# RWKV-7 + NSA trunk on one core: kk's head sums, their spread back and the gate branch's last 32 rows as 32-wide tiles on quarters of the array

## The reference, cut to what matters

```python
r = xr @ w_r;  k = xk @ w_k;  v = xv @ w_v
w_log = -softplus(-(w0 + tanh(xw @ wa) @ wb)) - 0.5
a = sigmoid(a0 + (xa @ aa) @ ab)
g = sigmoid(xg @ ga) @ gb                       # ga: 1024 x 160, gb: 160 x 1024
kk = heads(k * k_k)                             # 16 heads of 64
kk = kk / max(norm(kk over the head), 1e-12)
k = k * (1 + (a - 1) * k_a)
```

## Time and profile before

| | |
|---|---|
| median of 3 executions | 880.41 us (880.11 to 882.34) |
| the profiled execution | 882.25 us, of which the span in the trace is 880.5 us |
| PE busy | 809.8 us, 92% of the span |
| DVE / ACT / POOL busy | 75% / 48% / 16% |
| twelve projections and what stands between them | about 47 to 151 us of the span |
| scan over time | from about 151 us on |

### The profile page before, as it was taken

The page is one execution under the profiler, slowest core; times in us unless marked ns, Lnnn a source line. Parts: engine busy times, 40 slices in busy tenths (PEclk is TensorE's granted clock), DMA queues, the critical chain, the costliest instruction groups (busy, mean ns, idle before and its releaser), DMA issues.

```text
span 880.5 us, 17952 instructions
## 1 busy us (share of the span) xinstructions
PE 809.8 (92%) x7613; PEld 699.9 (79%) x7613; DVE 663.1 (75%) x727; ACT 420.2 (48%) x596; POOL 138.4 (16%) x207
## 2 busy tenths in 40 slices
PE   0899999899989899999999989998889899999997
PEld 0598899787877599999998788975566799999975
DVE  4897987998977689999997674789854687555552
ACT  2269532654553734434444654238646454444441
POOL 8700014534621300000000041101110000000000
PEclk9999999999999999999999999989999999999999
DMA  8953225423250859999993586670005276655541
GB/s 312 335 167 112 85 97 172 176 99 113 99 205 1 311 211 374 378 377 376 377 366 123 192 254 202 187 256 1 1 2 190 99 283 241 192 191 191 191 144 48
DMA packets 71838, 170.18 MB, mean 193 GB/s; under 512 B 5432, under 2 KB 6736, under 8 KB 71760
## 3 DMA queue, kind: packets, MB, share of 16 engines
q1 hardware_dynamic: 68784, 160.75, 52.2%
q0 software_dynamic: 2416, 7.15, 2.7%
q10 hardware_dynamic: 560, 1.14, 0.3%
HBM read 166.42 MB, written 1.05 MB: 190 GB/s over the span
## 4 chain that ended last, share of the span: by engine, by line
PE 66%; DVE 22%; ACT 7%; issue 3%; DMA 2%; ACTq 0%; POOL 0%; DVEq 0%; POOLq 0%
PE ps L1724 8%; PE ps L1727 8%; PE ps L1726 8%; PE ps L1735 7%; PE ps L1737 7%; PE ps L1739 7%; DVE wlo L1070 4%; PE ps L1670 2%; PE ps L1672 2%; PE ps L1673 2%; DVE acc L1042 2%; ACT whi L638 2%; PE ps L1841 2%; DVE hfull L1354 1%; DVE tt L1241 1%
## 5 line engine op out<-in xcount | busy, mean ns | idle before, releaser
L1070 DVE TENSOR_TENSOR wlo<-raw,whi 128x2048 fp32r<-128x2048 f32 (+1 forms) x98 | 217.2, 2216 | 55.4 <-ACT whi L638 53.2
L638 ACT ACTIVATE whi<-raw 128x2048 fp32r<-128x2048 f32 (+1 forms) x98 | 179.8, 1843 | 135.1 <-DMA raw<-in_mlp_down_dram 87.5
L1724 PE MATMUL ps<-ghi,whi 128*128 128x256 f32 x576 | 164.8, 286 | 8.0 <-ACT ghi L884 4.3
L1726 PE MATMUL ps<-glo,whi 128*128 128x256 f32 x576 | 164.4, 285 | 0.0
L1727 PE MATMUL ps<-ghi,wlo 128*128 128x256 f32 x576 | 164.3, 285 | 0.0
L1724 PEld LDWEIGHTS ps<-ghi,whi 128*128 128x128 f32 x576 | 111.9, 194 | 11.3 <-issue 7.6
L1726 PEld LDWEIGHTS ps<-glo,whi 128*128 128x128 f32 x576 | 112.1, 195 | 0.5
L1727 PEld LDWEIGHTS ps<-ghi,wlo 128*128 128x128 f32 x576 | 112.0, 194 | 0.0
L1735 PE MATMUL ps<-whi,hidhi 128*128 128x512 f32 x256 | 100.8, 394 | 2.0 <-DVE wlo L1070 2.0
L1737 PE MATMUL ps<-whi,hidlo 128*128 128x512 f32 x256 | 99.8, 390 | 0.0
L1739 PE MATMUL ps<-wlo,hidhi 128*128 128x512 f32 x256 | 99.6, 389 | 0.0
(11 more groups left out here) (358 smaller groups left out, 1593.4 us busy)
## 6 DMA issues: line engine op xcount, KB each, us to landing
raw<-in_mlp_up_dram SPq DMA_DIRECT2D x32, 1024.0 KB, 5.5
raw<-in_mlp_down_dram SPq DMA_DIRECT2D x32, 1024.0 KB, 5.2
raw<-in_ada_w_dram SPq DMA_DIRECT2D x24, 1024.0 KB, 6.0
late<-in_ada_w_dram SPq DMA_DIRECT2D x24, 1024.0 KB, 9.0
late<-in_kv_ada_w_dram SPq DMA_DIRECT2D x8, 1024.0 KB, 8.3
raw<-in_kv_w_dram SPq DMA_DIRECT2D x6, 1024.0 KB, 5.3
raw<-in_rw_k_dram SPq DMA_DIRECT2D x4, 1024.0 KB, 8.8
raw<-in_rw_r_dram SPq DMA_DIRECT2D x4, 1024.0 KB, 5.0
```

Of the source, the lines that this page charges most:

```text
L638: ins = sc.activation(whi[i][:, ks, :], raw[i][:, :].rearrange("p (k n) -> p k n", k=4)[:, ks, :], ACT.Copy)
L1070: ins = dv.tensor_tensor(wlo[i][:, ks, :], raw[i][:, :].rearrange("p (k n) -> p k n", k=4)[:, ks, :], whi[i][:, ks, :].bitcast(F32), ALU.s ...
L1724: mm(out_, whi[b][:, k, cols], hi[:, k0 + k, :], start=(first and k == 0 and m % 2 == 0), stop=False, skip_group_check=True)
L1726: mm(out_, whi[b][:, k, cols], lo[:, k0 + k, :], start=False, stop=False, skip_group_check=True)
```

## The change

It touches four small products and the tables that they use:

- the head sums go to four column tiles of 32 (output partitions 0, 32, 64, 96): pair j of heads goes with the table `indq` (128 x 2 x 32) to tile j // 2, so four tiles take two matmuls each, ordered by quarters (0, 2, 4, 6, 1, 3, 5, 7);
- root, clamp and reciprocal work on 128 partitions instead of 16;
- the spread takes 32 rows of `s16` per matmul (row tiles), in the same order; `indt` becomes 128 x 2 x 128;
- `gate_inner` computes the last 32 rows four times, once into each quarter of bank 5: 32 matmuls instead of 8;
- `gate_outer` replaces `lora_outer` for the gate: first the 8 matmuls with gb0, then 8 with 32 rows of gb1 each, a quarter of the array each; gb1 is loaded four times, once into each quarter (four DMAs instead of one);
- the memsets of s16, tg1 and gb1 go, and SyncE's wait for s_const ahead of gb0 goes; low_rank(0) and gate_inner wait for 8 small loads instead of 5.

```diff
-        indt = at("indt", [P, D], F32, 196.5)
+        indt = at("indt", [P, 2, P], F32, 196.5)
+        indq = at("indq", [P, 2, 32], F32, 197.5)
...
-                    sp.wait_ge(s_const, 1)
                     sp.dma_start(gb0[:, :], A["rw_gb"][0, 0:P, :]).then_inc(s_lora_out, 16)
-                    sp.dma_start(gb1[0:32, :], A["rw_gb"][0, P:160, :]).then_inc(s_lora_out, 16)
+                    for c in range(4):
+                        sp.dma_start(gb1[32 * c:32 * c + 32, :], A["rw_gb"][0, P:160, :]).then_inc(s_lora_out, 16)
...
-            st.do(g.memset(s16[:, :], 0.0))
-            st.do(g.memset(tg1[:, :], 0.0))
-            st.do(g.memset(gb1[:, :], 0.0))
...
+            st.do(g.memset(indq[:, :, :], 0.0))
...
+                st.do(g.memset(indq[rows, :, :].rearrange("p j c -> p (j c)")[:, e:e + 35:34], 1.0))
...
-            st.do(g.memset(indt[:, :], 1.0))
-            select(indt[:, :], 0, [[1, D]], -64)
-            select(indt[:, :], 63, [[-1, D]], 64)
+            st.do(g.memset(indt[:, :, :], 0.0))
+            for c in range(4):
+                select(indt[32 * c:32 * c + 32, :, :].rearrange("p j (e d) -> p j e d", e=2), 0,
+                       [[-2, 2], [-1, 2], [0, N]], 1, ALU.not_equal, 1.0)
...
-            sc.activation(tg1[0:32, :], ps[0:32, 5, 0:S], ACT.Sigmoid).then_inc(s_t1, 1)
+            sc.activation(tg1[:, :], ps[:, 5, 0:S], ACT.Sigmoid).then_inc(s_t1, 1)
...
-            sc.activation(s16[0:H, :], ps[0:H, 6, 0:S], ACT.Sqrt).then_inc(s_kks, 1)
+            sc.activation(s16[:, :], ps[:, 6, 0:S], ACT.Sqrt).then_inc(s_kks, 1)
...
-            st.do(dv.tensor_scalar(s16[0:H, :], s16[0:H, :], 1e-12, None, ALU.max))
-            st.tell(dv.reciprocal(s16[0:H, :], s16[0:H, :]), T["kk"])
+            st.do(dv.tensor_scalar(s16[:, :], s16[:, :], 1e-12, None, ALU.max))
+            st.tell(dv.reciprocal(s16[:, :], s16[:, :]), T["kk"])
...
+            BY_QUARTERS = (0, 2, 4, 6, 1, 3, 5, 7)
...
-                pe.wait_ge(s_lora_out, 16 * 5)
-                for b, m0, m1 in ((4, 0, P), (5, P, 160)):
-                    for k in range(KC):
-                        ins = mm(ps[0:m1 - m0, b, 0:S], ga[:, k, m0:m1], tmpF[:, k, :], start=(k == 0), stop=(k == KC - 1))
+                pe.wait_ge(s_lora_out, 16 * 8)
+                for k in range(KC):
+                    mm(ps[:, 4, 0:S], ga[:, k, 0:P], tmpF[:, k, :], start=(k == 0), stop=(k == KC - 1))
+                for k in range(KC):
+                    for c in range(4):
+                        ins = mm(ps[32 * c:32 * c + 32, 5, 0:S], ga[:, k, P:160], tmpF[:, k, :], start=(k == 0),
+                                 stop=(k == KC - 1))
                 ins.then_inc(s_l1, 1)
...
+            def gate_outer():
+
+                for j in range(KC):
+                    mm(ps[:, 4 + j // 2, (j % 2) * S:(j % 2) * S + S], gb0[:, P * j:P * j + P], tg0[:, :],
+                       start=(j % 2 == 0), stop=False, skip_group_check=True)
+                for j in BY_QUARTERS:
+                    rows = slice(32 * (j // 2), 32 * (j // 2) + 32)
+                    ins = mm(ps[:, 4 + j // 2, (j % 2) * S:(j % 2) * S + S], gb1[rows, P * j:P * j + P], tg1[rows, :],
+                             start=False, stop=True, skip_group_check=True)
                 ins.then_inc(s_l2, 1)
...
-            for j in range(KC):
-                ins = mm(ps[0:H, 6, 0:S], ind[:, j, :], gF[:, j, :], start=(j == 0), stop=(j == KC - 1))
+            for j in BY_QUARTERS:
+                ins = mm(ps[16 * j - 16 * (j % 2):16 * j - 16 * (j % 2) + 32, 6, 0:S], indq[:, j % 2, :], gF[:, j, :],
+                         start=(j % 2 == 0), stop=(j % 2 == 1))
             ins.then_inc(s_kk_ps, 1)
...
-            for j in range(KC):
-                ins = mm(ps[:, 4 + j // 2, (j % 2) * S:(j % 2) * S + S], indt[:, P * j:P * j + P], s16[:, :],
+            for j in BY_QUARTERS:
+                rows = slice(32 * (j // 2), 32 * (j // 2) + 32)
+                ins = mm(ps[:, 4 + j // 2, (j % 2) * S:(j % 2) * S + S], indt[rows, j % 2, :], s16[rows, :],
                          start=True, stop=True)
...
-            lora_outer([(gb0, tg0[:, :]), (gb1, tg1[:, :])])
+            gate_outer()
```

More of the change, by code:

```diff
@@ L1635, in gate_inner, with lora_outer @@
                 pe.wait_ge(s_mix, 5)
-                pe.wait_ge(s_lora_out, 16 * 5)
-                for b, m0, m1 in ((4, 0, P), (5, P, 160)):
-                    for k in range(KC):
-                        ins = mm(ps[0:m1 - m0, b, 0:S], ga[:, k, m0:m1], tmpF[:, k, :], start=(k == 0), stop=(k == KC - 1))
+                pe.wait_ge(s_lora_out, 16 * 8)
[5 more added lines that the diff above has]
+                                 stop=(k == KC - 1))
                 ins.then_inc(s_l1, 1)
-            def lora_outer(parts):
+            def lora_outer(w, x):
                 for j in range(KC):
-                    out_ = ps[:, 4 + j // 2, (j % 2) * S:(j % 2) * S + S]
-                    for n, (w, x) in enumerate(parts):
-                        ins = mm(out_, w[:, P * j:P * j + P], x, start=(n == 0), stop=(n == len(parts) - 1))
+                    ins = mm(ps[:, 4 + j // 2, (j % 2) * S:(j % 2) * S + S], w[:, P * j:P * j + P], x, start=True, stop=True)
+                ins.then_inc(s_l2, 1)
+            def gate_outer():
[6 more added lines that the diff above has]
+                             start=False, stop=True, skip_group_check=True)
                 ins.then_inc(s_l2, 1)
@@ L1653, in low_rank @@
                 else:
-                    pe.wait_ge(s_lora_out, 16 * 5)
+                    pe.wait_ge(s_lora_out, 16 * 8)
                     pe.wait_ge(s_t1, 1)
-                lora_outer([(wab[rows, :], twa[rows, :])])
+                lora_outer(wab[rows, :], twa[rows, :])
             def parts_ready(q):
```

## The result

The changed kernel takes 886.91 us (median of 20 runs, 876.43 to 890.44), the kernel before 880.99 beside it (20 runs, 877.64 to 884.73): a ratio of 1.0051, 95% interval 1.003 to 1.0073, so slower by half a per cent. 876.1 us, faster, was predicted.

A forecast was written before the change was run, and what follows sets the result against it. TensorE was taken to bound the changed stretch, with VectorE and then POOL late next. The profiled 882.25 us less 4.3 gives 877.95; taken off the 880.41 median, 876.1 us, range 874.2 to 879.4 (own range 875.0 to 877.4, chance 0.67).

The forecast's parts named there:

- Tiles four at a time: Changed small products on TensorE: four 32-wide tiles run side by side, so each narrow stage takes about 1.2 us, not 3.6.
- The new wait of TensorE ahead of gate_outer: After projection(6), TensorE ends at 110.6 us and waits 0.9 us for VectorE's KK_NORMED at 111.5.
- GpSimd as the releaser of the masks: At the scan's begin, GpSimd's (POOL's) sv ends at 149.05 us and releases the masks at 149.1 instead of 153.37.
- Three more loads at no cost: SP's queue ahead of k's last piece: 2.9 us issue, at most 3.9 traffic, 7.2 cover, so 0.
- its signs of being wrong: gate_inner 10 us or more; masks released by TensorE; POOL's sv before 147; a load wait between 45 and 60 us.
- what is late next: Section from the shortened TensorE stages through VectorE and POOL to the masks, giving -4.3 us, carried to the end.
- the sum's -4.3: Masks at the scan's begin start at 149.1 us instead of 153.37; -4.3 us taken off the whole time.
- GpSimd's term: Ahead of the masks, POOL's 9.26 us of work after kr(3) loses 1.9 of TensorE's 6.1 us.
- the 6.1 us of TensorE: At the end of the projections, TensorE is through at 145.0 us instead of 151.18, 6.1 us sooner.
- the 7.0 us on TensorE: TensorE's list: head sums -2.6, spread -2.2, gate_outer -2.2, gate_inner 0; together -7.0 us.
- the scan's own chain takes up the 4.3 us: Rival, in the scan: ScalarE's later begin or the wait at its end absorbs the gain; 880.4 us; chance 0.06.
- The rival of column tiles in turn: Rival: column tiles run one at a time, gate_inner +10.4 us, head sums gain nothing; 886.4 us; chance 0.06.

The follow-up runs named there:

- a1_again: The changed kernel unaltered, measured a second time against the kernel before: 887.10 us, ratio 1.0072.
- g1: The changed kernel plus 40 small matmuls in TensorE's idle time at 10 us, constants not moved: 880.58 us, ratio 0.9997 to the kernel before.
- h3: The changed kernel plus 40 small matmuls at 10 us, constants not moved, measured again: 877.95 us, ratio 0.9978 to the kernel before.
- f3: The kernel before plus 24 small matmuls in TensorE's idle time at 10 us, none of the change: 891.21 us, ratio 1.012 to the kernel before.
- f4: The changed kernel with GpSimd's output-parity constants made before its wait, plus 40 small matmuls at 10 us: 874.89 us, ratio 0.9925 to the kernel before.
- h2: The changed kernel with early output-parity constants and 40 small matmuls at 10 us, measured again on another chip: 876.76 us, ratio 0.9961 to the kernel before.
- h1: The changed kernel's tiled head sums and spread, gate branch from the kernel before, early output-parity constants, no padding: 875.95 us, ratio 0.9951 to the kernel before.
- g3: The changed kernel with early output-parity constants plus 24 small matmuls at 10 us: 882.78 us, ratio 1.0003 to the kernel before.
- g2: The kernel before plus 64 small matmuls at 10 us, one whole 16 KB of instructions: 883.48 us, ratio 1.0034 to the kernel before.
- h4: The kernel before plus 64 small matmuls at 10 us, measured again: 880.71 us, ratio 1.0007 to the kernel before.

## Why the prediction was wrong

**Right, each by its row.** Tiles four at a time, in both kinds. gate_inner 82.17 to 89.41, 7.24 us. Each narrow stage 1.1 us. The new wait of TensorE ahead of gate_outer: 0.74 us, 0.9 forecast. VectorE's kkF without idle time, at 107.79 instead of 109.91. GpSimd as the releaser of the masks, with parity between; from gate_inner's start to sv's end the forecast has 65.5 us and the trace 65.5. Three more loads at no cost: ScalarE's copy waited for nothing. The trace does not bear out the rule of the Trainium skill on weight loads (page "TensorE: Matmul & The Clock Gate", section "Part 3: Packing small matmuls — row/col tiling"): the 64 column tiles share all their rows and yet start 0.052 us apart, and by the rule gate_inner would have taken 10.4 us more. All the signs that the prediction listed lie ahead of 150 us, and none of its signs of being wrong appeared: it had no sign for what happened in the scan.

**The step that failed** is the last of the section on what is late next: "From there VectorE, TensorE and the ring of weights release each other, nothing is tied to an absolute time, and I carry -4.3 to the end". Two things are tied to something else. TensorE's own program is fetched in blocks of 16 KB through the same DMA engines as the weights, and where a block ends is set by how many instructions stand ahead of it; gate_inner's 48 extra matmul records and their loads moved that, and TensorE stopped three times for 1.24, 2.56 and 3.99 us at block boundaries. I costed gate_inner's quadrupling at 0 because only 16 slots are filled, and counted no price for instructions. On the changed kernel that was worth 5 to 9 us: by the means 4.5 and 6.4 us over before with the place as it fell (the result, a1_again), 0.6 and 3.0 us under it with the place restored (g1, h3); on the kernel before the same place cost 9.6 us (f3). The second is the wait at the masks itself: TensorE stood idle behind GpSimd's constants and its clock fell, which took 1.3 to 2.0 us at the scan's begin.

With the place restored and nothing else, the sum's -4.3 still isn't reached: g1 and h3 have it at the masks (4.4 and 4.8 us ahead), half clock takes 1.3 of it, and late in the scan 2.7 and 3.5 us are left. With the constants early too, GpSimd's term is gone and the prediction's own list would give the 6.1 us of TensorE: f4 and h2 are 5.6 and 6.1 us ahead at the masks and end 6.3 and 3.6 us below before by the medians. h1, with -4.8 of the 7.0 us on TensorE, is 4.4 below. So the sum is right up to the masks, and what was carried to the end was not.

The rival "the scan's own chain takes up the 4.3 us" had the right stretch with another mechanism and no loss beyond zero; no rival ended slower through the scan, and 0.06 for slower was too little. The rival of column tiles in turn names 886.4 us, close to the 886.91 measured; that is chance, since gate_inner took 7.24 us and not the 17.6 that it rests on.

**What stays open.** Why only some boundaries stop TensorE, and for how long: a block late by 3 to 4 us and a dense run of 64x64 matmuls behind it are present at both long stops, but how far ahead a block is asked for no row tells, and the same boundary stopped one kernel for 2.94 and for 3.99 us. g3 shows that the good places can't be read off one number. g2's 1.0034 against h4's 1.0007 stays unexplained. And behind 570 us, at the attention's begin, executions differ by some 4 us at the lower clock: f4's profiled run goes from 7.5 us ahead of before to 2.6 and ends 4.3 ahead, h2's, the same kernel, goes from 8.4 to 8.3. It may be much of the spread of each kernel's runs, which only the profiled ones can show, and it touches both kernels.

## What to carry to other kernels

Count instructions as well as slots: quadrupling a matmul over four tiles is free on the array and still moves every later instruction of TensorE's program against its 16 KB blocks. Where DMA is full and TensorE runs short matmuls, compare a local gain with the program's length kept (padded to a whole block in idle time, or by using only the parts that add nothing) before judging it. Stops put down to "issue" in the middle of a group, with a packet of the instruction queue 2 to 3 us ahead of their end, are the sign. That the stop stands at the same count of instructions in another version of the kernel, and not at the same line, is the stronger one.

## What the runs showed that was not expected

The same kernel before, with 24 tiny matmuls in an idle stretch of 11 us, is 1.2% slower; with 64 of them it was 2.6 and 0.5 us over before in the mean (g2, h4), so they themselves cost little or nothing. A block that comes in a gap between weight loads lets TensorE go on 2.2 us later (216.7 to 218.90), at the other stop 2.1 to 2.6. Of the fourteen stops of 2 us or more in the runs' traces, eleven had the granted clock at 0.5, that is 1.2 GHz, at their end or behind it for several microseconds, which added to the loss: in a1_again 190 to 194, 221 to 224 and 245 to 252 us. The two of 2.56 us and the one of 2.75 had not, and the stop of 1.24 us had it in the changed kernel (173 to 180 us) and in f3, but not in a1_again. 16 row tiles of 32 rows or 16 column tiles of 32 columns took 1.15 and 1.07 us where the whole array took 3.62 and 3.63.
